# Gathering and the first expert's products in turns, in a mixture-of-experts kernel

## The chip, the cores and the metric

One NeuronCore of a Trainium2 chip runs one program. The metric is the device time of one execution in microseconds (us); lower is better. Engines are named as in the profile: PE is TensorE (PEld its weight loads), ACT is ScalarE, DVE is VectorE, POOL is GpSimd, SP is the queue that issues the weight loads. Each engine works through its own instructions strictly in program order and waits on semaphores for the others.

## The reference, cut to what matters

A trunk of four layers on 384 tokens (128 context, 256 latent) of width 1024. Each layer has a token mixer (gated DeltaNet, grouped-query attention, latent attention, DeltaNet again) and then a mixture of experts. Both are wrapped in a modulation before and a LayerNorm after. The part that the change touches is the mixture:

```python
def _moe(h, router_w, router_b, w_gate, w_up, w_down):
    scores = sigmoid(t @ router_w)                        # 16 experts, 4 groups of 4
    best_group = argmax(sum of the top-2 biased scores)   # one group for each token
    e_idx = top-2 experts inside the best group
    hid = silu(einsum("td,edf->tef", t, w_gate)) * einsum("td,edf->tef", t, w_up)
    out = einsum("tef,efd->td", hid * combine[..., None], w_down)
```

The LayerNorm is `(x - mean) * rsqrt(var + eps) * g + b` of `ALPHA * x + (1 + gate) * f(h)`.

## The kernel before, in words

**Layout.** Activations lie features by tokens: 128 partitions, 8 feature tiles, 384 columns. `bufh` holds the modulated input of a sub-layer, `bufo` the normalised values before their scale, `bufx` the residual.

**Two-part numbers.** Products of the experts are made from 32-bit values that are split into a high part (rounded to the fp32r type) and a low part (the rest). ACT copies a weight piece into `e_whi` (`split_high`, L2074, the copy's own line is L1675), then DVE subtracts it from the weight and writes `e_wlo` (`split_low`, L2802, instruction L2806). For each feature tile PE makes three products (L1495, L1498, L1499): high by high, high by low, low by high.

**Routing.** Tokens of one group are packed together. After LayerNorm, PE makes the router scores and transposes the tokens (L1555), DVE finds the group and each token's slot (`route`, L2661 to L2760), and a one-hot matrix `e_pick` says which token goes to which slot. Then every engine reads a flag and branches around a path for crowded groups (in this data the branch is not taken). DVE's first instruction after this branch is a wait at L2874.

**Gathering.** `gather_piece` (PE, L1436, instruction L1451) multiplies tokens by `e_pick`. There are eight pieces for the first pair of groups (`("G", 0, m)`). Piece m covers the feature pair q = m mod 4; pieces 0 to 3 are of the high parts, 4 to 7 of the low parts. Each is six matmuls into PSUM bank 5 or 6, and `gathered_piece` (ACT, L2059) copies the bank to `e_hs`. A piece may start when the one two before it has been copied.

**The order of the work** is the list `MOE_STEPS` for PE: first all eight `G` steps, then `U` of expert 0 (four pieces of `gate_up`, L1528, two feature tiles each, 24 column products of 512), then `W` (`pair_weights`, L1455, instruction L1462), then `U` of expert 1, and so on with `D` (down products), `T` (transposes) and `S` (scatter). ACT and DVE both follow `MOE_FOLLOW`, made from that list: `("P", j, e, p)` is the split of weight piece p, `("g", ...)` a copy of a gathered piece. Copies wait in `_open` until two pieces of the next expert stand in the list, so it begins with P0, P1, then g0 to g7, then P2, P3, P4, P5. Three pieces of split weights fit (`SPLITS`): the split of piece p waits until piece p - 3 has been used.

**Weights from memory** are loaded by SP into `ring`, eight units of 1 MB (a unit holds two pieces). A unit is loaded again when PE has used it (`ring_free`). `MOE_UNITS` is the order of these loads.

**The residual.** `scale_residual(n)` on POOL (L2924) writes ALPHA times the normalised values to `bufx`, eight instructions (L2935), one for each feature tile. It waits first for all of the next sub-layer's modulated input (`wait_all_h`, L586, called at L2932), which ACT (five tiles) and DVE (three tiles, L2252, six instructions) write, and then for each tile's `normed`, which DVE's multiply by the root (L2245) signals. It is called seven times with n above 0.

Of the kernel before, what the change touches and what calls it, by code (L numbers as in the profile page):

```python
# [28 lines left out]
P = 128  # L29
# [14 lines left out]
NE, NG, EPG = 16, 4, 4  # L44
# [48 lines left out]

MOE_STEPS = [("G", 0, m) for m in range(8)]
for _x in range(NE):
    _group, _turn = divmod(_x - 6, EPG)
    _late = _x >= 6 and _turn < 2
    if _x == 8:  # L100
        MOE_STEPS.append(("W", 1, 0))
    MOE_STEPS.append(("U", _x // EPG, _x % EPG))
    if _x == 0:
        MOE_STEPS.append(("W", 0, 0))
    if _x in (4, 5):
        MOE_STEPS += [("G", 1, 4 * (_x - 4) + m) for m in range(2)]
    if _late:
        MOE_STEPS.append(("S", _group, 2 * _turn))
    if _x >= 2:
        MOE_STEPS.append(("D", (_x - 2) // EPG, (_x - 2) % EPG))  # L110
    if _x in (4, 5):
        MOE_STEPS += [("G", 1, 4 * (_x - 4) + m) for m in range(2, 4)]
    if _late:
        MOE_STEPS.append(("S", _group, 2 * _turn + 1))
    if _x >= 1:
        MOE_STEPS.append(("T", (_x - 1) // EPG, (_x - 1) % EPG))
MOE_STEPS += [("D", 3, 2), ("T", 3, 3), ("D", 3, 3)] + [("S", 3, q) for q in range(4)]

MOE_UNITS = [(j, e, part) for kind, j, e in MOE_STEPS if kind in "UD" for part in ((0, 1) if kind == "U" else (2,))]


PIECE = UNIT // 2
# [4 lines left out]
MOE_FOLLOW, MOE_PIECE_OF = [], {}  # L127
_open, _p = [], 0
for _kind, _j, _e in MOE_STEPS:
    if _kind in "UD":  # L130
        for _k in range(4 if _kind == "U" else 2):
            MOE_FOLLOW.append(("P", _j, _e, _p))
            MOE_PIECE_OF[_kind, _j, _e, _k] = _p
            _p += 1
            if _k == 1:
                MOE_FOLLOW += _open
                _open = []
    if _kind == "W":
        _open.insert(0, ("w", _j, _e, None))
    elif _kind != "D":  # L140
        _open.append((_kind.lower(), _j, _e, None))
    elif _e == EPG - 1:
        _open.append(("y", _j, _e, None))
MOE_FOLLOW += _open
MOE_PIECES = _p
# [215 lines left out]
def trunk(nc, I, O):  # L361

    unit_at, n_units = unit_plan()
    with ExitStack() as ctx:
# [78 lines left out]
        c = Carve()  # L443
# [142 lines left out]
        def wait_all_h(eng, n):  # L586
            wait_h(eng, n, H_ACT - 1)
            wait_h(eng, n, KT - 1)
# [140 lines left out]
        def _(pe):  # L729
# [703 lines left out]
                      lambda h, kt: m_v[:, h // 2 % 2, kt, P * (h % 2):P * (h % 2) + P], fill, lambda p: None)  # L1433


            def gather_piece(l, pair, m):  # L1436

                at = 16 * l + 8 * pair + m
                half, q = divmod(m, 4)
                if m == 0:  # L1440
                    pe.wait_ge(F["pick"], 2 * l + pair + 1)
                    pe.wait_ge(tk_hi, 2 * TT * (l + 1))
                if m == 4:
                    pe.wait_ge(tk_lo, 2 * TT * (l + 1))
                if m >= 2:
                    pe.wait_ge(F["ga_ev"], at - 1)
                out = ps[:, 5 + q % 2, :].rearrange("p (g f c) -> p g f c", g=2, f=2)
                for f in range(2):
                    ft = 2 * q + f
                    for t in range(TT):  # L1450
                        last = mm(out[:, :, f, :], (e_hi, e_lo)[half][:, t, P * ft:P * ft + P], e_pick[:, t, :],  # L1451
                                  start=(t == 0), stop=(t == TT - 1))
                last.then_inc(F["ga"], 1)

            def pair_weights(l, pair, comb):  # L1455

                pe.wait_ge(comb_ready, l + 1)
                pe.wait_ge(row2_ready, l + 1)
                for g in range(2):
                    at = EPG * (2 * pair + g)  # L1460
                    for t in range(TT):
                        last = mm(ps[:, 7, 96 + 4 * g:100 + 4 * g], e_pick[:, t, P * g:P * g + P].bitcast(F32),  # L1462
                                  comb[:, t, at:at + EPG], start=(t == 0), stop=(t == TT - 1))
                last.then_inc(cs_mm, 1)
# [75 lines left out]
            def moe(l):  # L1540
# [84 lines left out]
                for kind, j, e in MOE_STEPS:  # L1625
                    n = NE * l + EPG * j + e
                    if kind == "G":
                        gather_piece(l, j, e)
                    elif kind == "W":
                        pair_weights(l, j, comb)  # L1630
                    elif kind == "U":
                        if e == 0 and j % 2 == 0:
                            pe.wait_ge(F["ga_ev"], 16 * l + 8 * (j // 2) + 8)
                        for k in range(4):
                            p = MOE_PIECE_OF["U", j, e, k]
                            gate_up(F, MOE_PIECES * l + p, p, HS_OF[j], e, k)
                    elif kind == "T":
                        transpose_hidden(F, n, e % 2)
                    elif kind == "D":
                        pe.wait_ge(F["thi"], n + 1)  # L1640
                        pe.wait_ge(F["tlo"], n + 1)
                        for k in range(2):
                            p = MOE_PIECE_OF["D", j, e, k]
                            down(F, MOE_PIECES * l + p, p, e, k)
                    else:
                        n = NG * l + j
                        if e == 0:
                            pe.wait_ge(F["ga_ev"], 16 * l + 16)
                        scatter_piece(F, n, e, e_put[:, j % 2, :], (6, 0, 1, 2) if j == NG - 1 else (5, 6),
                                      n * KT if n else None)  # L1650
# [19 lines left out]
        def _(act):  # L1670
# [385 lines left out]
                sweep(l, lambda n: m_root[:, n % TT:n % TT + 1], fill, lambda p: None)  # L2056


            def gathered_piece(l, pair, m):  # L2059
                at = 16 * l + 8 * pair + m  # L2060
                half, q = divmod(m, 4)
                act.wait_ge(F["ga"], at + 1)
                slots = e_hs[:, 0:2] if pair == 0 else e_hs[:, 0:3:2]
                copy(slots[:, :, half, 2 * q:2 * q + 2, :].rearrange("p g f c -> p g (f c)"),
                     ps[:, 5 + q % 2, :].rearrange("p (g c) -> p g c", g=2)).then_inc(F["ga_ev"], 1)

            def gathered_block(n):
                for half in range(2):
# [851 lines left out]
        def _(pool):  # L2920
# [3 lines left out]
            def scale_residual(n):  # L2924

                if n == 0:
                    wait_all_h(pool, 0)
                    for k in range(KT):
                        last = G.tensor_scalar(bufx[:, k, :], bufx[:, k, :], ALPHA, None, ALU.mult)
                    last.then_inc(ax_ready, 1)  # L2930
                    return
                wait_all_h(pool, n)  # L2932
                for k in range(KT):
                    pool.wait_ge(normed, KT * (n - 1) + k + 1)
                    last = G.tensor_scalar(bufx[:, k, :], bufo[:, k, :], x_gb[:, 0, KT * (n - 1) + k:KT * (n - 1) + k + 1],  # L2935
                                           x_gb[:, 1, KT * (n - 1) + k:KT * (n - 1) + k + 1], ALU.mult, ALU.add)
                last.then_inc(ax_ready, 1)
# [208 lines left out]
```

## Time and profile before

| what | value |
|---|---|
| three runs | 2209.02, 2210.88, 2216.32 us, median 2210.88 |
| the profiled execution's own time | 2213.71 us |
| its span, first to last instruction | 2211.9 us |
| PE busy | 2038.2 us, 92% of the span |
| DVE busy | 1339.1 us, 61% |
| ACT busy | 1034.5 us, 47% |
| POOL busy | 244.0 us, 11% |
| mean granted PE clock | 0.966 of full speed |

An engine is busy while an instruction of it runs. The granted clock is 1.00 at PE's full 2.4 GHz and 0.50 at 1.2 GHz. The gathering of the four layers begins at 510.36, 915.94, 1364.46 and 2004.63 us of the span.

### The profile page before, as it was taken

To read this page: it belongs to the slowest core of one execution; us is meant where nothing else is said; L and a number is where in the kernel's file an instruction comes from. 1 tells how busy PE (TensorE), PEld (TensorE's weight loads), DVE (VectorE), ACT (ScalarE), POOL (GpSimd) and SP (SyncE) were. 2 spreads that over 40 slices of the span, in tenths; PEclk is the share of its full clock that TensorE was granted. 3 is DMA by queue.
4 is the path that set the end of the run, shared out by engine and by line. 5 is a ranking of instruction groups with operands and counts; after the bars stand their busy time and mean duration, and the time that the engine had idled before them with its cause. 6 is when DMAs were issued, how large, how long until landed. Compare 5 with 4: busy or idle time off the path is not lost.

```text
span 2211.9 us, 44967 instructions
## 1 busy us (share of the span) xinstructions
PE 2038.2 (92%) x18880; PEld 1420.3 (64%) x18881; DVE 1339.1 (61%) x2625; ACT 1034.5 (47%) x1783; POOL 244.0 (11%) x363
## 2 busy tenths in 40 slices
PE   6999999898998999899899998998899999988996
PEld 3566666557775665677666665776466666647774
DVE  2566655437896341689722325898656666437896
ACT  3344444226774341576523315765444454226773
POOL 0432222110001000100010001000322232100000
PEclk9999999998999999899999998999999999889998
DMA  9234343345895444488643443887311121025880
GB/s 378 95 131 173 121 151 148 142 153 186 284 318 203 164 173 163 145 310 297 236 151 142 152 172 131 309 303 267 117 45 64 45 69 64 26 79 181 281 299 29
DMA packets 56768, 381.22 MB, mean 172 GB/s; under 512 B 6384, under 2 KB 10480, under 8 KB 12000
## 3 DMA queue, kind: packets, MB, share of 16 engines
q1 hardware_dynamic: 51552, 373.00, 47.2%
q10 hardware_dynamic: 4608, 4.20, 0.5%
q8 instruction: 159, 2.61, 0.5%
q0 software_dynamic: 384, 0.89, 0.1%
q14 instruction: 65, 0.53, 0.1%
HBM read 373.96 MB, written 4.10 MB: 171 GB/s over the span
## 4 chain that ended last, share of the span: by engine, by line
PE 77%; DVE 13%; ACT 5%; issue 3%; DMA 1%; SPq 0%; ACTq 0%; DVEq 0%
PE ps L834 15%; PE ps L1495 6%; PE ps L1499 5%; PE ps L1498 5%; DVE e_wlo L2806 5%; PE ps L786 4%; PE ps L762 4%; PE ps L742 3%; PE ps L974 3%; PE ps L1282 3%; DVE bufx L2824 2%; PE ps L797 2%; ACT e_whi L1675 2%; PE ps L1451 2%; PE ps L1383 2%
## 5 line engine op out<-in xcount | busy, mean ns | idle before, releaser
L2806 DVE TENSOR_TENSOR e_wlo<-ring,e_whi 128x1024 fp32r<-128x1024 f32 x384 | 456.0, 1220 | 94.6 <-ACT e_whi L1675 79.2
L1675 ACT ACTIVATE e_whi<-ring 128x1024 fp32r<-128x1024 f32 x384 | 402.9, 1060 | 120.4 <-PE ps L1499 117.2
L834 PE MATMUL ps<-bufh,ring 128*128 128x384 f32 x1024 | 394.7, 507 | 6.9 <-ACT bufo L1731 4.7
L834 PEld LDWEIGHTS ps<-bufh,ring 128*128 128x128 f32 x1024 | 177.3, 192 | 98.3 <-issue 23.3
L1495 PE MATMUL ps<-e_whi,e_hs 128*128 128x512 f32 x512 | 210.7, 412 | 28.3 <-DVE e_wlo L2806 24.8
L1675 ACT ACTIVATE scratch<-ps 128x384 f32<-128x384 f32 (+6 forms) x311 | 109.1, 368 | 220.5 <-PE ps L834 52.4
L1499 PE MATMUL ps<-e_whi,e_hs 128*128 128x512 f32 x512 | 200.8, 392 | 0.0
L1498 PE MATMUL ps<-e_wlo,e_hs 128*128 128x512 f32 x512 | 199.9, 390 | 0.0
L2935 POOL TENSOR_SCALAR bufx<-bufo,x_gb 128x384 f32<-128x384 f32 x56 | 36.2, 661 | 1104.3 <-DVE bufh L2252 1104.3
L1495 PEld LDWEIGHTS ps<-e_whi,e_hs 128*128 128x128 f32 x512 | 96.0, 188 | 69.2 <-ACT e_whi L1675 41.8
L2338 DVE SCALAR_TENSOR_TENSOR scratch<-scratch,par 128x386 f32<-128x386 f32 x192 | 128.4, 669 | 4.8
L742 PE MATMUL ps<-ring,silc 128*32 128x128 f32 x3072 | 105.8, 292 | 20.1 <-DMA ring<-in_w_ada 20.1
L1675 ACT ACTIVATE scratch<-ps,scratch 128x128 f32<-128x128 f32 x96 | 31.8, 365 | 194.6 <-PE ps L1129 192.9
L1495 PE MATMUL ps<-e_whi,e_hidT 128*128 128x512 f32 x256 | 103.2, 403 | 13.3 <-issue 9.2
L1499 PEld LDWEIGHTS ps<-e_whi,e_hs 128*128 128x128 f32 x512 | 96.0, 188 | 21.9
L742 PEld LDWEIGHTS ps<-ring,silc 128*32 128x32 f32 x3072 | 87.8, 117 | 33.8 <-DMA ring<-in_w_ada 15.6
L1498 PEld LDWEIGHTS ps<-e_wlo,e_hs 128*128 128x128 f32 x512 | 96.4, 188 | 16.6
L1675 ACT ACTIVATE lnt<-ps 128x384 f32<-128x384 f32 x26 | 12.7, 490 | 195.5 <-PE ps L797 178.6
L1498 PE MATMUL ps<-e_wlo,e_hidT 128*128 128x512 f32 x256 | 102.2, 399 | 0.0
L1499 PE MATMUL ps<-e_whi,e_hidT 128*128 128x512 f32 x256 | 101.7, 397 | 0.0
L974 PEld LDWEIGHTS ps<-scratch 32*32 32x32 f32 x6144 | 64.8, 107 | 54.7 <-issue 37.2
L2224 DVE SCALAR_TENSOR_TENSOR bufh<-ps,mod,bufx 128x128 f32<-128x128 f32 x64 | 23.4, 412 | 118.9 <-PE ps L762 77.3
(312 smaller groups left out, 3525.1 us busy)
## 6 DMA issues: line engine op xcount, KB each, us to landing
ring<-in_moe SPq DMA_DIRECT2D x192, 1024.0 KB, 4.9
ring<-in_w_ada SPq DMA_DIRECT2D x96, 1024.0 KB, 6.8
ring<-in_gdn_w_in SPq DMA_DIRECT2D x32, 1024.0 KB, 6.6
ring<-in_gdn_w_out SPq DMA_DIRECT2D x8, 1024.0 KB, 4.8
ring<-in_gqa_w_in SPq DMA_DIRECT2D x6, 1024.0 KB, 4.8
ring<-in_gqa_w_out SPq DMA_DIRECT2D x4, 1024.0 KB, 6.7
ring<-in_mla_w_out SPq DMA_DIRECT2D x4, 1024.0 KB, 7.8
ring<-in_mla_w_in SPq DMA_DIRECT2D x3, 1024.0 KB, 4.9
```

Of the source, the lines that this page charges most:

```text
L742: last = mm(ps[32 * g:32 * g + 32, bank, 0:P], silc[:, kt, :], w[:, k, g, :], start=(kt == 0), stop=(kt == KT - 1))
L762: last = mm(ps[:, banks[t % len(banks)], 0:T], w[:, t % 2, kt, :], rhs[:, kt, :], start=(kt == 0), stop=(kt == KT - 1))
L786: last = mm(ps[:, banks[t % len(banks)], 0:T], w[:, t % 2, kt, :], bufo[:, kt, :], start=(kt == 0), stop=(kt == KT - 1))
L834: last = mm(ps[:, head_bank(n, m), 0:T], w[:, m % 2, kt, :], bufh[:, kt, :], start=(kt == 0), stop=(kt == KT - 1))
L974: last = mm(ps[quarter(g), bank, at:at + 32], g_inv[a][quarter(g), d, t, :], g_inv[b][quarter(g), d, t, :], start=True, stop=True)
L1282: last = mm(ps[:, bank, 0:T], w[:, pos % 2, kt, :], bufh[:, kt, :], start=(kt == 0), stop=(kt == KT - 1))
L1495: first = mm(out, parts[0], whi, start=start, stop=False)
L1498: mm(out, parts[0], wlo, start=False, stop=False)
L1499: return mm(out, parts[1], whi, start=False, stop=stop)
L1675: return op(out, in_, ACT.Copy, **kw)
L2338: done = stt(acc, g_cin[:, m, tap:tap + CONVW], taps[:, tap:tap + 1], acc, ALU.mult, ALU.add)
L2806: return tt_(e_wlo[:, b, :], w, e_whi[:, b, :].bitcast(F32), ALU.subtract)
```

## The change

PE's order for expert 0 of each layer is now G0 G1 V0, G2 G3 V1, G4 G5 V2, G6 G7 V3, where `("V", 0, k)` is the piece k of expert 0's gate and up products. The eight gathering pieces come in the order 0, 4, 1, 5, 2, 6, 3, 7, so that the high and the low part of one feature pair stand side by side, and V k needs just these two. The lists of ACT and DVE become g0 g1 P0, g2 g3 P1, g4 g5 P2, g6 g7 P3, then P4, P5 as before. `V` waits for the copies of its two pieces. The order of the loads from memory stays the same. Apart from this, `scale_residual` no longer waits for the whole modulated input (for n above 0), only for each tile's `normed`.

```diff
--- before.py
+++ after.py
@@ -93,13 +93,15 @@
 
 
 
-MOE_STEPS = [("G", 0, m) for m in range(8)]
+GATHER_ORDER = ((0, 4, 1, 5, 2, 6, 3, 7), tuple(range(8)))
+MOE_STEPS = [step for k in range(4) for step in (("G", 0, 2 * k), ("G", 0, 2 * k + 1), ("V", 0, k))]
 for _x in range(NE):
     _group, _turn = divmod(_x - 6, EPG)
     _late = _x >= 6 and _turn < 2
     if _x == 8:
         MOE_STEPS.append(("W", 1, 0))
-    MOE_STEPS.append(("U", _x // EPG, _x % EPG))
+    if _x:
+        MOE_STEPS.append(("U", _x // EPG, _x % EPG))
     if _x == 0:
         MOE_STEPS.append(("W", 0, 0))
     if _x in (4, 5):
@@ -116,7 +118,8 @@
         MOE_STEPS.append(("T", (_x - 1) // EPG, (_x - 1) % EPG))
 MOE_STEPS += [("D", 3, 2), ("T", 3, 3), ("D", 3, 3)] + [("S", 3, q) for q in range(4)]
 
-MOE_UNITS = [(j, e, part) for kind, j, e in MOE_STEPS if kind in "UD" for part in ((0, 1) if kind == "U" else (2,))]
+MOE_UNITS = [(0, 0, 0), (0, 0, 1)]
+MOE_UNITS += [(j, e, part) for kind, j, e in MOE_STEPS if kind in "UD" for part in ((0, 1) if kind == "U" else (2,))]
 
 
 PIECE = UNIT // 2
@@ -127,6 +130,16 @@
 MOE_FOLLOW, MOE_PIECE_OF = [], {}
 _open, _p = [], 0
 for _kind, _j, _e in MOE_STEPS:
+    if _kind == "V":
+        MOE_FOLLOW.append(("P", 0, 0, _p))
+        MOE_PIECE_OF["U", 0, 0, _e] = _p
+        _p += 1
+        if _e == 3:
+            _open.append(("u", 0, 0, None))
+        continue
+    if _kind == "G" and _j == 0:
+        MOE_FOLLOW.append(("g", 0, _e, None))
+        continue
     if _kind in "UD":
         for _k in range(4 if _kind == "U" else 2):
             MOE_FOLLOW.append(("P", _j, _e, _p))
@@ -1433,18 +1446,18 @@
                       lambda h, kt: m_v[:, h // 2 % 2, kt, P * (h % 2):P * (h % 2) + P], fill, lambda p: None)
 
 
-            def gather_piece(l, pair, m):
-
-                at = 16 * l + 8 * pair + m
-                half, q = divmod(m, 4)
-                if m == 0:
+            def gather_piece(l, pair, n):
+
+                at = 16 * l + 8 * pair + n
+                half, q = divmod(GATHER_ORDER[pair][n], 4)
+                if n == 0:
                     pe.wait_ge(F["pick"], 2 * l + pair + 1)
                     pe.wait_ge(tk_hi, 2 * TT * (l + 1))
-                if m == 4:
+                if n == GATHER_ORDER[pair].index(4):
                     pe.wait_ge(tk_lo, 2 * TT * (l + 1))
-                if m >= 2:
+                if n >= 2:
                     pe.wait_ge(F["ga_ev"], at - 1)
-                out = ps[:, 5 + q % 2, :].rearrange("p (g f c) -> p g f c", g=2, f=2)
+                out = ps[:, 5 + n % 2, :].rearrange("p (g f c) -> p g f c", g=2, f=2)
                 for f in range(2):
                     ft = 2 * q + f
                     for t in range(TT):
@@ -1628,6 +1641,9 @@
                         gather_piece(l, j, e)
                     elif kind == "W":
                         pair_weights(l, j, comb)
+                    elif kind == "V":
+                        pe.wait_ge(F["ga_ev"], 16 * l + 2 * e + 2)
+                        gate_up(F, MOE_PIECES * l + e, e, HS_OF[0], 0, e)
                     elif kind == "U":
                         if e == 0 and j % 2 == 0:
                             pe.wait_ge(F["ga_ev"], 16 * l + 8 * (j // 2) + 8)
@@ -2056,13 +2072,13 @@
                 sweep(l, lambda n: m_root[:, n % TT:n % TT + 1], fill, lambda p: None)
 
 
-            def gathered_piece(l, pair, m):
-                at = 16 * l + 8 * pair + m
-                half, q = divmod(m, 4)
+            def gathered_piece(l, pair, n):
+                at = 16 * l + 8 * pair + n
+                half, q = divmod(GATHER_ORDER[pair][n], 4)
                 act.wait_ge(F["ga"], at + 1)
                 slots = e_hs[:, 0:2] if pair == 0 else e_hs[:, 0:3:2]
                 copy(slots[:, :, half, 2 * q:2 * q + 2, :].rearrange("p g f c -> p g (f c)"),
-                     ps[:, 5 + q % 2, :].rearrange("p (g c) -> p g c", g=2)).then_inc(F["ga_ev"], 1)
+                     ps[:, 5 + n % 2, :].rearrange("p (g c) -> p g c", g=2)).then_inc(F["ga_ev"], 1)
 
             def gathered_block(n):
                 for half in range(2):
@@ -2929,7 +2945,6 @@
                         last = G.tensor_scalar(bufx[:, k, :], bufx[:, k, :], ALPHA, None, ALU.mult)
                     last.then_inc(ax_ready, 1)
                     return
-                wait_all_h(pool, n)
                 for k in range(KT):
                     pool.wait_ge(normed, KT * (n - 1) + k + 1)
                     last = G.tensor_scalar(bufx[:, k, :], bufo[:, k, :], x_gb[:, 0, KT * (n - 1) + k:KT * (n - 1) + k + 1],
```

## Rows read from the trace of the kernel before

**Rows 1.** The page, busy time, share of the span, instructions: PE.

```profile
PE 2038.2 (92%) x18880; PEld 1420.3 (64%) x18881; DVE 1339.1 (61%) x2625; ACT 1034.5 (47%) x1783; POOL 244.0 (11%) x363
```

**Rows 2.** Timeline of layer 3's gathering and first expert: start, length, engine, line, count, idle before.

```profile
2004.13 1.28 ACT L1675 ACT_TABLE_LOAD   x1 [3.21 <-issue]
...
2004.63 2.90 PE L1451 MATMUL ps<-e_pick,e_hi 128*128 128x256 f32 x12 [4.24 <-issue]
...
2007.96 1.68 PE L1451 MATMUL ps<-e_pick,e_hi 128*128 128x256 f32 x12 [0.43 <-ACT e_hs L1675]
...
2009.71 3.33 PE L1451 MATMUL ps<-e_pick,e_lo 128*128 128x256 f32 x24
2010.64 2.36 DVE L2806 TENSOR_TENSOR e_wlo<-ring,e_whi 128x1024 fp32r<-128x1024 f32 x2 [3.38 <-DVEq L2873]
...
2012.36 1.32 ACT L1675 ACTIVATE e_hs<-ps 128x512 fp32r<-128x512 f32 x2 [0.34 <-PE ps L1451]
2013.58 1.05 ACT L1675 ACTIVATE e_whi<-ring 128x1024 fp32r<-128x1024 f32 x1
...
2013.73 0.50 PE L1495 MATMUL ps<-e_whi,e_hs 128*128 128x512 f32 x1 [0.69 <-ACT e_hs L1675]
...
2014.66 1.23 DVE L2806 TENSOR_TENSOR e_wlo<-ring,e_whi 128x1024 fp32r<-128x1024 f32 x1 [1.66 <-ACT e_whi L1675]
...
2017.95 2.52 DVE L2806 TENSOR_TENSOR e_wlo<-ring,e_whi 128x1024 fp32r<-128x1024 f32 x2 [0.22 <-ACT e_whi L1675]
...
2019.34 1.40 PE L1462 MATMUL ps<-lnt,e_pick 128*128 128x4 f32 x12
```

**Rows 3.** Timeline of layers 0 to 2: DVE's first split, PE's end of expert 0.

```profile
515.97 2.36 DVE L2806 TENSOR_TENSOR e_wlo<-ring,e_whi 128x1024 fp32r<-128x1024 f32 x2 [3.48 <-DVEq L2873]
...
525.83 1.40 PE L1462 MATMUL ps<-lnt,e_pick 128*128 128x4 f32 x12
...
921.98 2.36 DVE L2806 TENSOR_TENSOR e_wlo<-ring,e_whi 128x1024 fp32r<-128x1024 f32 x2 [3.41 <-DVEq L2873]
...
931.81 1.40 PE L1462 MATMUL ps<-lnt,e_pick 128*128 128x4 f32 x12
...
1370.12 2.36 DVE L2806 TENSOR_TENSOR e_wlo<-ring,e_whi 128x1024 fp32r<-128x1024 f32 x2 [3.40 <-DVEq L2873]
...
1379.66 1.40 PE L1462 MATMUL ps<-lnt,e_pick 128*128 128x4 f32 x12
```

**Rows 4.** Windows: stretch, length, busy of each engine, granted clock, DMA.

```profile
1532.50:1534.00 1.50, 0.41 (x2) 0.40 (x3) 1.50 (x5) 0.16 (x1) 0.00 (x0) 1.00 0.55 229
...
1975.00:1976.50 1.50, 0.38 (x4) 0.14 (x4) 1.50 (x3) 1.26 (x2) 0.00 (x0) 1.00 0.07 27
1976.50:1978.00 1.50, 1.50 (x10) 0.35 (x8) 1.28 (x2) 1.46 (x3) 0.00 (x0) 0.59 0.00 0
```

**Rows 5.** Waits of PE from 520 to 690 us: line, releaser, total, times, longest.

```profile
PE ps L1495 <- DVE e_wlo L2806: 6.1, 9, 1.1
```

**Rows 6.** Issues of weight loads by SP from 500 to 540 us.

```profile
L664 SPq DMA_DIRECT2D ring<-in_moe x6: 327/328/328, 522.1 to 538.1; - x6
```

**Rows 7.** Timeline of POOL and DVE after layer 0's first LayerNorm.

```profile
490.65 1.82 DVE L2252 TENSOR_SCALAR bufh<-bufo,h_gb 128x128 f32<-128x128 f32 x6
...
492.64 5.18 POOL L2935 TENSOR_SCALAR bufx<-bufo,x_gb 128x384 f32<-128x384 f32 x8 [48.62 <-DVE bufh L2252]
...
495.33 0.58 DVE L2673 TENSOR_TENSOR lnt<-lnt 128x24 f32<-128x24 f32 x1
495.83 0.17 DVE L2674 TENSOR_TENSOR lnt<-lnt 128x24 f32<-128x24 f32 x1
496.04 0.52 DVE L2677 TENSOR_TENSOR lnt<-lnt 128x12 f32<-128x12 f32 x1
...
496.75 0.45 DVE L2681 TENSOR_TENSOR lnt<-lnt 128x12 f32<-128x12 f32 x1
497.23 0.61 DVE L2683 TENSOR_TENSOR lnt<-lnt 128x12 f32<-128x12 f32 x1
```

## The prediction

> **What bounds the kernel now.** I read the page first: PE is busy 92% of the span and no other engine is near it [rows 1]. So the change can only give back PE's idle time, and it can cost time wherever it makes PE wait. Next I read the timeline of one gathering with the first expert behind it, in layer 3, line by line [rows 2], because the change reorders just this stretch, and then the same instants in layers 0 to 2 [rows 3].
>
> The reader should see four things in rows 2. First, the gathering is nearly a stream of PE work: 12 matmuls (two pieces) take 2.90 us at first and 1.68 us from 2007.96 on, and the stretch from 2004.63 to expert 0's first product at 2013.73 is 9.10 us long. Second, DVE starts its first low split only at 2010.64, 6.0 us after the gathering began. It waited for none of the others: its releaser is its own sequencer at L2873, the branch around the crowded path. Third, the splits of P0 and P1 are done in the shadow of the gathering, and P2 and P3 while PE multiplies with P0 and P1. So expert 0's products run almost without a stop from 2013.73 to 2019.34, 5.61 us, or 1.40 us a piece. Fourth, at each hand-over only one engine's latency is paid: a copy that ends at 2013.68 lets PE start at 2013.73.
>
> **The change part by part.**
>
> *The new order makes a chain.* No matmul is added or removed. But PE can go past V0 to G2 and G3 only when P0 is split, ACT splits P1 only after g3 is copied, and g3 needs PE to have finished G3, which stands behind V0. Queued behind the waiting V on PE are the next two gathering pieces, and ACT's next copy and split wait for these. So within a round nothing overlaps but the copy of the first piece of a pair. I add up a round from V(k-1)'s start to V(k)'s start, with durations of rows 2:
> - V(k-1): 1.40
> - the pair of gathering pieces: 1.68
> - from PE's end of the pair (2009.71 + 3.33 = 2013.04) to the end of the second copy (2012.36 + 1.32 = 2013.68): 0.64
> - high split, which starts 0.10 before the copy ends: 1.05 - 0.10 = 0.95
> - step to DVE 0.03, low split 1.23, step to PE 0.05: 1.31
>
> Together 5.98 us a round, in which PE stands still for 2.90 us (0.64 + 0.95 + 1.31).
>
> *The first round.* G0 and G1 end at 2004.63 + 2.90 = 2007.53. ACT's table load, which stood ahead of the first split at 2004.13, would be over at 2005.41 and stays free. Copies and high split of P0 are then done around 2009.1, but DVE comes at 2010.64 as before, since its branch isn't moved. V0 starts at 2010.64 + 1.23 + 0.05 = 2011.92, and V3 ends 3 x 5.98 + 1.40 = 19.34 us later, at 2031.26. Before, `W` began at 2019.34: 11.92 us lost. The same sum from DVE's start in the other layers [rows 3]: layer 0 515.97 gives 536.59 against 525.83, 10.76; layer 1 921.98 gives 942.60 against 931.81, 10.79; layer 2 1370.12 gives 1390.74 against 1379.66, 11.08. Sum of the four layers: **+44.6 us**, with PE at full clock.
>
> *The clock.* PE's clock falls when it has had little to do: it went from 1.00 to 0.50 in the window 1976.50 to 1978.00, after a window in which PE was busy 0.38 of 1.50 us and one like it before, while it stayed at 1.00 through 1532.50 to 1534.00, where PE was busy only 0.41 of 1.50 us but came from and went into dense work [rows 4]. The new rounds lie between the two: 3.1 us of dense work, then 2.9 us of nothing, four times, and 4.4 us of nothing ahead of V0 (2007.53 to 2011.92), at a clock that was half before the gathering began. At half clock a pair of gathering pieces takes 2.90 in place of 1.68 us, +1.22 [rows 2]. For a product piece no row at half clock exists: between nothing for waits that hide it and a doubling, +1.40, I take +1.3, as the products are wide and stand back to back. If all V and the three later pairs run at half clock: 4 x 1.3 + 3 x 1.22 = 8.9 us a layer, 35.4 in all. I take half of it, since each round's work should lift the clock part of the time and each gap should drop it: **+17.7 us**; the ends are 0 and 35.4.
>
> The Trainium skill (TensorE: Matmul & The Clock Gate, "HAM oscillation — how this bites in real kernels") says that long idle gaps of the array, repeated in every round of a loop, bring it back to the slow clock each time. By it alone the sum would take the whole 35.4 us; row 1532.50 shows a short gap survived, so I keep the half.
>
> *Weight splits ahead.* P4 and P5 now can be split during V3. Before, P4's low split began at 2017.95, well ahead of expert 1 (2019.34 plus 1.40 for `W`) [rows 2], so this gains nothing there. All waits of PE for low splits in layer 0's experts are 6.1 us in nine places [rows 5]; a fraction of one of them is the most that a head start could spare. I count nothing, bounds 0 to -1.1 a layer.
>
> *Loads.* The same units in the same order. SP issues its first new load at 522.1, when expert 0's products free unit 0 [rows 6]: the ring is full by then, so the lost time is not used for transfers and not given back by them. PE's list of waits in these experts names no DMA [rows 5]. Cost 0.
>
> *POOL's wait.* Now POOL's eight instructions (5.18 us from 492.64) start as soon as the first `normed` is there, some 5 us earlier, beside L2245 and L2252 instead of beside `route`. What sharing costs DVE in `route` can be read from [rows 7]: L2673 takes 0.58 us where L2674, of the same shape and without the hold, takes 0.17; L2677, L2681 and L2683 take 0.52, 0.45 and 0.61. Against 0.17 these four are 1.5 us longer, on the path to the first gathering. Moved away, this is up to 1.5 us gained in each of four layers, -6.0. Against it, six L2252 (1.82 us in all) now run beside POOL in seven LayerNorms. If each were held to the end of a POOL instruction (5.18/8 = 0.65 us), six would take 3.9 us, +2.1 a time, 14.6 in all; if only the first is held, at most 0.65. L2674 was let through directly behind a held one, so I take 0.8 a time, +5.6. The two nearly cancel: **0**, bounds -6 to +9 (14.6 - 6.0 = 8.6). Nobody waits for POOL's result earlier than before.
>
> The Trainium skill (GPSIMD Engine Reference, "Key points") says that GpSimd shares its SBUF interfaces with VectorE and contends with instructions that have two SBUF inputs or run in a two-port mode. The trace agrees for the first kind (0.58 against 0.17 us) [rows 7]; no row of this kernel shows L2252 beside POOL. By this rule L2252 may be held as well, which is the +9 end.
>
> Sum: 44.6 + 17.7 + 0 = 62.3 us. The profiled execution took 2213.71 us and its span 2211.9, 1 and 3 us above the median of the runs; on the profiled time it gives 2276, and on the median 2210.88 it gives **2273.2 us**, 2.8% slower.
>
> **The rivals.**
>
> *A. The chain at full clock* (0.19): the gaps of 2.9 us are survived as at 1532.50. 2210.9 + 44.6 = 2255.5. For it: dense work around each gap. Against it: the clock is already at half ahead of G0.
>
> *B. The chain at half clock all along* (0.23): 2210.9 + 44.6 + 35.4 = 2291. For it: the gaps repeat, and the first is 4.4 us. Against it: 1532.50 [rows 4].
>
> *C. The change does what its order suggests, faster* (0.04): the split of a piece is ready by the time PE reaches its V, so the products fill PE's waits in the gathering. Before, the stretch was 9.10 us long, of which the matmuls at their rate take 2.90 + 3 x 1.68 = 7.9; saving all of it is 1.2 us a layer, and with the POOL term 2210.9 - 4.8 - 6.0 = 2200.1. This decides if PE's wait ahead of each V is under some 0.3 us; my sum has 2.9. Against it: the list of ACT puts P(k) behind the copy for which PE was the only source.
>
> *D. The stall is made good later* (0.03): a fuller ring or splits done ahead remove waits of the later experts, 2211. Against it: only 6.1 us of such waits a layer, and the ring was full already [rows 5, 6].
>
> *E. A part of the chain overlaps in a way I don't see* (0.06), such as a shorter hand-over or the first round sooner: between +10 and +40, about 2236.
>
> **How the numbers follow.** The forecast (the chain, half of its work at half clock) has 0.45, A 0.19, B 0.23, C 0.04, D 0.03, E 0.06. The predicted time is the forecast's, 2273. The range reaches from A with the POOL gain and some waits spared (2248) to B with the whole POOL cost (2300). It leaves out C, D and most of E, and a little at the top. 0.3% (6.6 us) is about what a measurement of this kernel can tell from no change. Faster by more: C, 0.04. Within: D, 0.03. Slower: all the rest, 0.93.
>
> **What the changed profile would show.** Four times a layer PE idle ahead of L1495, released by DVE L2806, with about 2.9 us in rounds 1 to 3 and 4.4 us in the first; in PE's waits this pair rises by some 52 us (four times 4.4 + 3 x 2.9). Between the ends of V0 and V1 some 6 us at full clock and up to 8.6 at half. ACT idle ahead of `e_hs` copies, released by PE. DVE's first L2806 still 3.4 us behind its L2873. The start of `W` 11 to 20 us later from the start of the gathering. The granted clock near half in part of this stretch. POOL's L2935 begins within L2245; L2673 falls to about 0.17 us, and L2252 rises above its 1.82 us for six. The prediction is wrong if PE passes from G3 to V1 without a wait, or if the experts after the first run with fewer waits than before by a like amount.

## The result, and the profile after

The changed kernel takes 2282.09 us in the median of four runs (2281.18 to 2289.05), the kernel before 2210.1 on the same chip: ratio 1.0327, 95% interval 1.0299 to 1.0355, so 72 us slower. The forecast was 2273, its range 2248 to 2300.

The page after, its busy line. PE works as long as before give or take one per cent, the span is 68 us longer (line order as in [rows 1]):

```profile
span 2280.1 us, 44956 instructions
...
PE 2060.0 (90%) x18880; PEld 1436.8 (63%) x18881; DVE 1337.1 (59%) x2625; ACT 1033.2 (45%) x1783; POOL 245.9 (11%) x363
```

PE's 22 us more of busy time come with the same 18880 instructions: they ran slower. The rest is waiting. PE's waits for low splits over the whole span, before and after (line, releaser, total us, times, longest):

```profile
PE ps L1495 <- DVE e_wlo L2806: 24.8, 36, 1.1
...
PE ps L1508 <- DVE e_wlo L2822: 78.6, 53, 4.8
```

They rose by 54 us, where some 52 were forecast.

In the changed kernel L1508 is the first product of a piece, as L1495 was before, L2822 the low split (L2806), L1464 the gathering (L1451), L1475 the weights product (L1462), L1691 ACT's copies (L1675), L2950 POOL's scaling (L2935), L2268 the modulation (L2252). Layer 0's gathering and first expert after, on the timeline, to be laid beside [rows 2, 3]:

```profile
508.13 1.62 PE L1464 MATMUL ps<-e_pick,e_hi 128*128 128x256 f32 x6 [5.68 <-issue]
...
509.55 1.48 PE L1464 MATMUL ps<-e_pick,e_lo 128*128 128x256 f32 x6
...
511.07 0.60 ACT L1691 ACTIVATE e_hs<-ps 128x512 fp32r<-128x512 f32 x1 [0.68 <-PE ps L1464]
511.56 1.05 ACT L1691 ACTIVATE e_whi<-ring 128x1024 fp32r<-128x1024 f32 x1
513.50 1.22 DVE L2822 TENSOR_TENSOR e_wlo<-ring,e_whi 128x1024 fp32r<-128x1024 f32 x1 [3.47 <-DVEq L2889]
...
514.87 0.65 PE L1508 MATMUL ps<-e_whi,e_hs 128*128 128x512 f32 x1 [3.84 <-DVE e_wlo L2822]
...
518.60 0.87 PE L1464 MATMUL ps<-e_pick,e_lo 128*128 128x256 f32 x6
518.80 1.31 ACT L1691 ACTIVATE e_hs<-ps 128x512 fp32r<-128x512 f32 x2 [6.19 <-PE ps L1464]
520.00 1.05 ACT L1691 ACTIVATE e_whi<-ring 128x1024 fp32r<-128x1024 f32 x1
521.08 1.22 DVE L2822 TENSOR_TENSOR e_wlo<-ring,e_whi 128x1024 fp32r<-128x1024 f32 x1 [6.36 <-ACT e_whi L1691]
...
522.45 0.77 PE L1508 MATMUL ps<-e_whi,e_hs 128*128 128x512 f32 x1 [2.98 <-DVE e_wlo L2822]
...
530.89 0.47 PE L1508 MATMUL ps<-e_whi,e_hs 128*128 128x512 f32 x1 [2.98 <-DVE e_wlo L2822]
...
538.34 0.46 PE L1508 MATMUL ps<-e_whi,e_hs 128*128 128x512 f32 x1 [2.98 <-DVE e_wlo L2822]
...
540.55 2.56 PE L1475 MATMUL ps<-lnt,e_pick 128*128 128x4 f32 x12
```

The reader should see the same idle time, 2.98 us, ahead of V1, V2 and V3, always released by DVE's low split; ACT idle for 6.19 us until PE's gathering, and DVE idle for 6.36 us until ACT: three engines take turns. The sum had 2.90 for this gap. V0 begins one low split after DVE's branch, as worked out (513.50 + 1.22 + 0.15 us for the step to PE). The rounds are 7.58, 8.44 and 7.45 us long (514.87, 522.45, 530.89, 538.34) in place of 5.98, because a part of them ran at the lower clock. The windows of these rounds and of what follows them, after (columns as in [rows 4], last but two the granted clock):

```profile
514.87:522.45 7.58, 4.60 (x18) 3.85 (x19) 1.22 (x1) 2.14 (x3) 0.00 (x0) 0.73 0.00 0
522.45:530.89 8.44, 5.46 (x18) 4.61 (x19) 1.22 (x1) 2.14 (x3) 0.00 (x0) 0.63 0.37 124
530.89:538.34 7.45, 4.47 (x18) 3.84 (x19) 1.37 (x2) 3.54 (x5) 0.00 (x0) 0.77 0.00 0
538.34:540.55 2.21, 2.21 (x6) 1.75 (x7) 2.13 (x2) 1.77 (x2) 0.00 (x0) 0.63 0.40 70
540.55:545.00 4.45, 4.45 (x18) 4.06 (x17) 1.79 (x7) 1.33 (x2) 0.00 (x0) 0.50 0.49 203
545.00:550.00 5.00, 5.00 (x15) 3.90 (x14) 2.56 (x3) 2.11 (x2) 0.00 (x0) 0.59 0.54 170
```

The last two rows matter: the weights product and expert 1 still run at half clock, though PE no longer waits. In layers 2 and 3 it is the same (0.68 and 0.67 in the 10 us from the weights product on, 0.57 in layer 0), in layer 1 the clock was back at once (0.95).

To see where time went in all layers I read three starts in each layer from the timelines: DVE's first normalising multiply (N), the first gathering (G) and the weights product (W). Sums over the four layers in us, one profiled execution of each kernel; "order alone", "fillers" and the others are the experiments below, and the last column is layer 3's mixer, from layer 2's last N to layer 3's first:

```
kernel              N to G   G to W   W to next N   layer 3's mixer
before                91.1     61.2       723.7          423.9
changed               85.6    132.9       734.2          417.2
POOL alone            85.8     60.3       721.9          416.4
order alone           91.5    133.1       735.0          416.2
fillers               84.7    107.9       723.0          417.1
```

The routing stretch (N to G) is 5.5 us shorter, the gathering with the first expert (G to W) 71.7 us longer, the other experts 10.5 us longer. The last column is taken up at the end.

### The profile page after: what moved, and what is told of

It reads as the page before. It is cut to its first block, busy times and chain, and to the rows that moved or that the text cites. A ratio compares the mean times of both kernels' runs of the same rounds, so it can differ in the third digit from the quotient of the medians.

```text
span 2280.1 us, 44956 instructions
## 1 busy us (share of the span) xinstructions
PE 2060.0 (90%) x18880; PEld 1436.8 (63%) x18881; DVE 1337.1 (59%) x2625; ACT 1033.2 (45%) x1783; POOL 245.9 (11%) x363
## 4 chain that ended last, share of the span: by engine, by line
PE 74%; DVE 15%; ACT 5%; issue 4%; DMA 1%; SPq 0%; DVEq 0%; ACTq 0%
PE ps L847 14%; PE ps L1508 6%; DVE e_wlo L2822 6%; PE ps L1512 5%; PE ps L1511 5%; PE ps L799 4%; PE ps L775 4%; PE ps L755 3%; PE ps L987 3%; PE ps L1295 3%; DVE bufx L2840 2%; ACT e_whi L1691 2%; PE ps L810 2%; PE ps L1464 2%; PE ps L1396 2%
## 5 line engine op out<-in xcount | busy, mean ns | idle before, releaser
L2822 DVE TENSOR_TENSOR e_wlo<-ring,e_whi 128x1024 fp32r<-128x1024 f32 x384 | 456.1, 1221 | 166.8 <-ACT e_whi L1691 151.6
L1691 ACT ACTIVATE e_whi<-ring 128x1024 fp32r<-128x1024 f32 x384 | 402.2, 1059 | 129.1 <-PE ps L1512 126.2
L1508 PE MATMUL ps<-e_whi,e_hs 128*128 128x512 f32 x512 | 220.6, 431 | 78.9 <-DVE e_wlo L2822 78.6
L1512 PE MATMUL ps<-e_whi,e_hs 128*128 128x512 f32 x512 | 210.0, 410 | 0.0
L1511 PE MATMUL ps<-e_wlo,e_hs 128*128 128x512 f32 x512 | 209.1, 408 | 0.0
L1691 ACT ACTIVATE scratch<-ps 128x384 f32<-128x384 f32 (+6 forms) x311 | 109.1, 368 | 217.9 <-PE ps L847 52.8
L1508 PEld LDWEIGHTS ps<-e_whi,e_hs 128*128 128x128 f32 x512 | 100.8, 197 | 121.7 <-issue 64.0
L2950 POOL TENSOR_SCALAR bufx<-bufo,x_gb 128x384 f32<-128x384 f32 x56 | 37.6, 686 | 1137.1 <-DVE bufo L2261 1137.1
L1691 ACT ACTIVATE scratch<-ps,scratch 128x128 f32<-128x128 f32 x96 | 31.7, 364 | 189.5 <-PE ps L1142 187.8
L1512 PEld LDWEIGHTS ps<-e_whi,e_hs 128*128 128x128 f32 x512 | 101.5, 198 | 23.6
L1508 PE MATMUL ps<-e_whi,e_hidT 128*128 128x512 f32 x256 | 104.1, 407 | 13.1 <-issue 9.2
L1511 PEld LDWEIGHTS ps<-e_wlo,e_hs 128*128 128x128 f32 x512 | 101.8, 199 | 17.5
L1691 ACT ACTIVATE lnt<-ps 128x384 f32<-128x384 f32 x26 | 12.7, 490 | 196.2 <-PE ps L810 177.6
L987 PE MATMUL ps<-scratch 32*32 32x32 f32 x6144 | 76.4, 195 | 19.4 <-issue 14.3
```

The source lines that it names most:

```text
L987: last = mm(ps[quarter(g), bank, at:at + 32], g_inv[a][quarter(g), d, t, :], g_inv[b][quarter(g), d, t, :], start=True, stop=True)
L1508: first = mm(out, parts[0], whi, start=start, stop=False)
L1511: mm(out, parts[0], wlo, start=False, stop=False)
L1512: return mm(out, parts[1], whi, start=False, stop=stop)
L1691: return op(out, in_, ACT.Copy, **kw)
L2822: return tt_(e_wlo[:, b, :], w, e_whi[:, b, :].bitcast(F32), ALU.subtract)
```

## The experiments

Twelve kernels were run. "Changed" is 2282.1 us; the kernel before was timed beside each.

**POOL alone**, the kernel before with only this edit:

```diff
-                wait_all_h(pool, n)
                 for k in range(KT):
                     pool.wait_ge(normed, KT * (n - 1) + k + 1)
```

> The kernel before, with only POOL's wait for the modulated input taken away. Theory (the wait's removal is worth nothing): the four held instructions of the routing, 1.5 us a layer, are freed, 6 us in all, and the six modulating instructions of DVE take 2.7 us in place of 1.8 in seven LayerNorms, 6.3 us in all; the time is 2210 us within 3. Rival (it is a part of the loss): 2219 us or more. Other rival (it is a gain that the new order hides): 2204 us.

Measured 2202.23 against 2210.62 us, ratio 0.9958 (0.9941 to 0.9975): faster by 9.3 us, give or take 4. So the edit was a gain that the order hid, as the second rival had it. DVE's timeline in this kernel, beside [rows 7]:

```profile
492.05 2.71 DVE L2252 TENSOR_SCALAR bufh<-bufo,h_gb 128x128 f32<-128x128 f32 x6
497.34 0.21 DVE L2667 TENSOR_TENSOR lnt<-lnt,par 128x48 f32<-128x48 f32 x1 [2.59 <-ACT lnt L2099]
497.58 0.18 DVE L2673 TENSOR_TENSOR lnt<-lnt 128x24 f32<-128x24 f32 x1
...
497.90 0.17 DVE L2677 TENSOR_TENSOR lnt<-lnt 128x12 f32<-128x12 f32 x1
```

Both effects are there in the size I had given them: six L2252 take 2.71 us in place of 1.82, L2673 0.18 in place of 0.58. L2245, which has one input in PSUM, was not slowed beside POOL: eight take 3.81 us, as before (3.80). Yet the stretch N to G is 5.3 us shorter over four layers, where the two effects alone make some 2.5 (4 x 1.5 less 4 x 0.9).

**The order alone**, the changed kernel with that wait put back:

```diff
+                wait_all_h(pool, n)
                 for k in range(KT):
```

> The changed kernel with POOL's wait put back, so that only the new order of gathering, products and splits is left. Theory: all of the loss is in the order, so 2282 us within 4, and the stretch from the first gathering to the weights product L1475's line is 32 to 34 us long in each layer, as in the changed kernel. Rival (POOL beside DVE costs a part): 2275 us or less.

2291.02 us, ratio 1.0366 (1.0340 to 1.0392): 81 us slower than before, 9 more than the whole change. Loss and gain add up, 81 - 9 = 72. The theory's place for the loss held (G to W is 133.1 us, 33.3 a layer), its 2282 for the total didn't, since it took POOL's part for nothing.

**Fillers.** Matmuls that nothing reads, in the gaps:

```diff
+FILLERS = (18, 22, 22, 22)
...
                     elif kind == "V":
+                        for x in range(FILLERS[e]):
+                            mm(ps[:, 1, 0:2 * P], e_hi[:, x % TT, 0:P], e_pick[:, x % TT, :], start=True, stop=True)
                         pe.wait_ge(F["ga_ev"], 16 * l + 2 * e + 2)
```

> The changed kernel with matmuls added that nothing reads: 18 of 256 columns ahead of V0 and 22 ahead of each of V1, V2 and V3, into a PSUM bank that is free there. They fill PE's idle time ahead of each product piece (4 and 2.98 us) and change no wait for splits. Theory (a part of the loss is the clock at half level, about 71 - 45 = 27 us, and the rest is the chain): granted clock 1.00 from the second round on, rounds of 6.0 us in place of up to 8.4, time 2282 - 24 = 2258 us within 6. Rival (the clock is a bystander and the loss is the chain's hand-overs alone): 2282 us or, with the matmuls in the way, more.

2244.8 us, ratio 1.0154 (1.0126 to 1.0181): 37 us less than changed, with 84 more matmuls a layer. That is 13 us below what was expected, which had 24 us for the clock; the rival, by which nothing would come back, is out. The timeline and two windows of this kernel:

```profile
514.84 0.47 PE L1509 MATMUL ps<-e_whi,e_hs 128*128 128x512 f32 x1 [1.43 <-DVE e_wlo L2825]
...
517.74 2.80 PE L1647 MATMUL ps<-e_pick,e_hi 128*128 128x256 f32 x22
...
520.88 0.47 PE L1509 MATMUL ps<-e_whi,e_hs 128*128 128x512 f32 x1 [0.35 <-DVE e_wlo L2825]
...
526.91 0.47 PE L1509 MATMUL ps<-e_whi,e_hs 128*128 128x512 f32 x1 [0.35 <-DVE e_wlo L2825]
...
532.96 0.47 PE L1509 MATMUL ps<-e_whi,e_hs 128*128 128x512 f32 x1 [0.35 <-DVE e_wlo L2825]
```

```profile
520.00:526.00 6.00, 5.65 (x42) 5.22 (x41) 1.19 (x2) 2.14 (x3) 0.00 (x0) 1.00 0.54 175
526.00:532.00 6.00, 5.65 (x42) 5.22 (x42) 1.18 (x2) 2.58 (x4) 0.00 (x0) 1.00 0.00 0
```

The rounds are 6.04, 6.03 and 6.05 us: the chain at full clock, which the sum put at 5.98. The clock is 1.00. With POOL alone as the base, this kernel shows the chain by itself: 1.0154/0.9958 = 1.0197, 43.5 us, give or take 7 by the two intervals; the sum had 44.6.

**Fillers ahead of V3 alone**, `FILLERS = (0, 0, 0, 22)`.

> The changed kernel with 22 matmuls that nothing reads ahead of V3 alone, none ahead of V0, V1 and V2. Theory (the half clock after V3 slows the weights product and expert 1 and costs 10 us of the clock's 36): V3, the weights product and expert 1 run at full clock, the stretch from the weights product to the LayerNorm falls from 183.5 to 181 us in each layer, and 2282 - 12 = 2270 us. Rival (that stretch is longer for another reason, the splits or the ring): no change there, 2280 us.

2264.49 us, ratio 1.0240 (1.0202 to 1.0277): 17.6 us less than changed, more than was expected. G to W is 130.7 us, 2.2 less than in the changed kernel, and W to next N is 719.2, 15.0 less. So the half clock carried past V3 was the larger part of what these 22 matmuls gave back; but as fillers ahead of every V left that stretch at 723.0, some 4 us of it vary from kernel to kernel. In this kernel the weights product is at full rate right behind V3:

```profile
542.68 0.47 PE L1509 MATMUL ps<-e_whi,e_hs 128*128 128x512 f32 x1
...
544.12 1.39 PE L1476 MATMUL ps<-lnt,e_pick 128*128 128x4 f32 x12
```

**Splits ahead.** PE's order as changed, the lists of ACT and DVE set by hand:

```diff
 MOE_PIECES = _p
+MOE_FOLLOW[:12] = [P0, P1, P2, g0, g1, g2, g3, P3, g4, g5, g6, g7]
```

(each entry written out as its tuple).

> The changed kernel with PE's order untouched, but ACT and DVE split P0, P1 and P2 ahead of all copies and P3 behind g3. Theory (the chain is long because each split stands behind the copies): the wait ahead of V1 to V3 falls from 2.98 to 0.7 us, a round from 6.0 to 3.8 us at full clock; V3 ends 20 us after the first gathering, 5.3 us later than before the change; with the clock mostly full after the first round, 2210 + 21 = 2231 us, at most 2245. Rival (PE's order itself, a product between two pairs, is what costs, whatever the splits do): above 2260 us.

2233.79 us, ratio 1.0097 (1.0073 to 1.0120): 48 us less than changed. The wait ahead of V1 is now for the copy, 0.69 us, and a round at full clock is 3.78 us (527.47 to 531.25; expected 3.8):

```profile
518.21 0.77 PE L1509 MATMUL ps<-e_whi,e_hs 128*128 128x512 f32 x1 [4.11 <-DVE e_wlo L2823]
...
523.69 0.50 PE L1509 MATMUL ps<-e_whi,e_hs 128*128 128x512 f32 x1 [0.69 <-ACT e_hs L1692]
...
527.47 0.50 PE L1509 MATMUL ps<-e_whi,e_hs 128*128 128x512 f32 x1 [0.69 <-ACT e_hs L1692]
...
531.25 0.50 PE L1509 MATMUL ps<-e_whi,e_hs 128*128 128x512 f32 x1 [0.69 <-ACT e_hs L1692]
```

**One pair ahead on PE**, the lists of ACT and DVE as changed:

```diff
-MOE_STEPS = [step for k in range(4) for step in (("G", 0, 2 * k), ("G", 0, 2 * k + 1), ("V", 0, k))]
+MOE_STEPS = [G0, G1, G2, G3, V0, G4, G5, V1, G6, G7, V2, V3]
...
+MOE_FOLLOW[:12] = [g0, g1, P0, g2, g3, P1, g4, g5, P2, g6, g7, P3]
```

> The changed kernel with the lists of ACT and DVE untouched (each split behind its copies), but PE one pair ahead: G0 G1 G2 G3 V0 G4 G5 V1 G6 G7 V2 V3. Theory (it is the closed circle of gathering, copy, split and product that costs): the copies and the split of the next piece go on beside a product, V3 ends about 18 us after the first gathering in place of 32 to 34, 2210 + 13 = 2223 us within 8. Rival (the splits behind the copies cost whatever PE does): above 2250 us.

2216.3 us, ratio 1.0030 (1.0011 to 1.0048): of the change's 72 us, 66 are gone by letting PE run two gathering pieces ahead, though each split still stands behind its copies. It keeps the POOL edit, so against POOL alone it is 1.0072, some 16 us. The circle is what cost most, and either cut opens it. What stays is in G to W again, 78.2 us against 60.3 of POOL alone (88.6 in splits ahead): PE still waits there, 15.4 us in the four layers against 3.3.

**Pieces in the shadow**: POOL's wait as before, PE's order `G0 G1 G2 G3 G4 G5 G6 V0 G7 V1 V2 V3`, lists `P0 P1 g0 ... g6 P2 g7 P3`.

> The new order of features, with POOL's wait as before, but PE's order G0 to G6, V0, G7, V1, V2, V3 and the splits P0 and P1 ahead of the copies, P2 behind g6, P3 behind g7. Theory (products can start before the last copy only if no split stands in the circle): the 0.7 us of PE's wait ahead of expert 0 goes, and DVE's first low split at 6.0 us is then nearly the bound; 0.5 us a layer, 2208 us within 3, which is no difference. Rival (products among gathering pieces cost by themselves): 2215 us or more.

2207.52 against 2211.47 us, ratio 0.9975 (0.9960 to 0.9990): a small gain of about 5.5 us. The profiled execution was the slowest of the twelve (2212.13 us), so it can't show where the gain lies: G to W is 62.8 us in it against 61.2 before. Its layers differ with the clock: 14.1 us in layer 0, where the half clock ended 3.7 us behind the first gathering, 16.1 to 16.6 in the others, where it lasted 7.7 to 9.6 us. So layers compare only where the half clock ended alike. Where it ended 3.5 to 3.8 us behind the first gathering, G to W is 13.9 to 14.1 us with these orders (layer 0 here, layers 1 to 3 of the run with POOL's wait removed as well, further down) and 14.4 to 14.6 with the order of before (layer 3 of POOL alone, layers 0 and 3 of the run with POOL's wait away ahead of the experts only). That is some 0.4 us a layer, near the 0.5 expected; where the rest of the 5.5 us comes from stays open.

**POOL behind e_pick**, the kernel before with one more wait ahead of the experts:

```diff
                 wait_all_h(pool, n)
+                if n % 2:
+                    pool.wait_ge(F["pick"], n)
```

> The kernel before, in which POOL's eight instructions in the LayerNorm ahead of the experts wait in addition until DVE has made e_pick, so that they run beside neither the routing's small instructions nor the modulation. Theory (DVE's instructions with two SBUF inputs are held by POOL, 1.5 us a layer on the path to the first gathering): 2210 - 6 = 2204 us within 3. Rival (the path to the gathering is set by something else): 2210 us.

2201.9 us, ratio 0.9960 (0.9942 to 0.9977), as much as POOL alone. Here six L2252 take 1.82 us and L2673 0.18. N to G is 83.9 us, 7.2 less than before.

**POOL's wait away ahead of the experts only** (`if n % 2 == 0: wait_all_h(pool, n)`), and **ahead of the mixers only** (`if n % 2: ...`).

> The kernel before, with POOL's wait taken away only in the four LayerNorms ahead of the experts. Theory (the gain is the routing's held instructions): the whole gain of the removal, 2203 us within 3, and with the three others left alone perhaps a little less. Rival (POOL's earlier end helps the mixers): 2210 us.

> The kernel before, with POOL's wait taken away only in the three LayerNorms ahead of a mixer. Theory (nothing there waits for POOL, and DVE's six modulating instructions take 0.9 us longer each time, part of it on the path): 2211 to 2213 us, no difference. Rival (this is where the gain came from): 2205 us or less.

Ahead of the experts: 2199.54 us, ratio 0.9947 (0.9929 to 0.9966), 11.7 us. Ahead of the mixers: 2209.19 us, ratio 0.9987 (0.9965 to 1.0010), no difference. So the gain comes from the wait in the four LayerNorms ahead of the experts. N to G is 83.1 us with it away there, 8.0 less than before, and 92.8 with it away ahead of the mixers only.

**Both together**: pieces in the shadow with POOL behind e_pick, and with POOL's wait removed.

> The last two together: pieces in the shadow and POOL behind e_pick. Theory: the two gains add, 2202 us within 4. Rival: the earlier gathering meets DVE's branch end, so that only one of them counts, 2206 us.

> Pieces in the shadow of the gathering, as in the run with G0 to G6, V0, G7, V1, V2, V3, together with the change's removal of POOL's wait. Theory: the removal is worth the 9 us that it was worth alone, and the pieces 4: 2198 us within 4, the same as with POOL behind e_pick. Rival (both shorten the same path): 2203 us.

2197.78 us, ratio 0.9938 (0.9916 to 0.9960), and 2195.75 us, ratio 0.9945 (0.9925 to 0.9965). Both are faster than both kernels, by 12 to 14 us against the one before; they don't differ from each other, nor clearly from POOL's wait away ahead of the experts alone.

## Why the prediction was right, step by step

**The chain** was right in kind and size. A round was put at 5.98 us with a gap of 2.90; measured 6.04 at full clock and gaps of 2.98. The sum of 44.6 us stands against 43.5 by the runs, and 46.7 by the stretch G to W (107.9 with fillers, less 61.2). Splits ahead and one pair ahead show that the circle made most of it, and not the placing of a product among gathering pieces.

**The clock** was right in kind and too small: 17.7 us taken, 37.3 measured (2282.1 - 2244.8), just over the upper end of 35.4. The term was mis-sized twice. Inside the rounds, G to W shrinks from 132.9 to 107.9 with fillers: 25.0 us where I had 17.7. And the term stopped at V3, while the half clock didn't: W to next N is 734.2 against 723.0 us, 11.2 us more. In layer 0 the clock was at 0.50 from 539 to 549 us, through the weights product (2.56 us in place of 1.40) and most of expert 1's gate and up products. The end of 35.4 was itself a little high: a product piece at half clock, six matmuls 0.43 us apart, takes 2.56 us, +1.16 in place of the +1.3 taken, which makes 33.2 us for all rounds at half. Against this the 25.0 say that some three quarters of the rounds' work ran at half clock, where I took half.

The reading of [rows 4] on which I took the half doesn't hold either. I wrote that PE came to 1532.50 from dense work; the window just before it shows that it didn't (first the one ahead of the row 1975.00, then this one):

```profile
1973.50:1975.00 1.50, 0.69 (x2) 0.08 (x1) 0.77 (x1) 0.00 (x0) 0.00 (x0) 1.00 1.03 437
...
1531.00:1532.50 1.50, 0.29 (x3) 0.06 (x1) 1.50 (x4) 1.17 (x2) 0.00 (x0) 1.00 0.91 382
```

PE was busy 0.70 of 3.00 us there and the clock stayed at 1.00; in the 3.00 us ahead of 1976.50 it was busy 1.07 us, and the clock fell. These rows don't tell which gaps are survived, so the half was a guess between the two ends. The Trainium skill (TensorE: Matmul & The Clock Gate, "HAM oscillation — how this bites in real kernels") tells of a loop whose waits of some 3 to 5 us bring the clock down in each round. Here the waits inside the rounds were 2.98 us, and the trace agrees in part: the windows of the three rounds have 0.73, 0.63 and 0.77, so the clock fell again and again, but not for the whole of a round. That 37.3 lies near the 35.4 that I had as the end by this rule is chance, since 11.2 of it came from behind the rounds.

**POOL's wait** was the step that failed: 0 taken with -6 as its end, -9.3 measured (interval -13 to -5.5). Its two parts had the right size on DVE, the hold on the routing gone and +0.9 us on the six modulating instructions. But it was counted in seven LayerNorms (at 0.8 each), and with the wait away ahead of the mixers only, no cost shows (0.9987). And the sum left out PE's clock between N and G.

PE's first product that needs the routing (L1570, in the changed kernel L1583) waits for DVE's `e_rs`. Its wait before, four times 3.1 us in the mean:

```profile
PE ps L1570 <- DVE e_rs L2696: 12.5, 4, 3.3
```

and after, 1.7, as in POOL alone:

```profile
PE ps L1583 <- DVE e_rs L2712: 6.9, 4, 1.7
```

The wait is shorter from both sides: `e_rs` comes some 0.6 us sooner, and the work ahead of it on PE ends some 0.9 us later, since it needs the modulated input. In POOL alone L1570 so starts 2.5 us earlier behind N, over four layers. The rest is in PE's matmuls from L1570 on, until DVE's L2726 starts, which waits for a part of them. These are layer 1's windows, before:

```profile
905.04:910.25 5.21, 5.21 (x25) 5.21 (x26) 2.95 (x10) 1.79 (x3) 0.00 (x0) 0.50 0.00 0
```

and in POOL alone:

```profile
901.16:905.03 3.87, 3.87 (x25) 3.56 (x26) 2.96 (x10) 1.74 (x3) 0.00 (x0) 0.76 0.00 0
```

Over the four layers this stretch takes 5.21, 5.21, 5.21 and 3.53 us before, and 4.45, 3.87, 5.21 and 2.80 in POOL alone, at granted clocks of 0.50, 0.50, 0.50, 0.76 and 0.62, 0.76, 0.50, 1.00: 2.8 us less with the same work. 2.5 and 2.8 are the 5.3 of N to G. No run changed the clock there by itself, but the profiles sort by the wait ahead of L1570: in the four kernels with 2.8 to 3.5 us of it in every layer (the one before, order alone, pieces in the shadow, wait away ahead of the mixers) the four stretches take 19.2 to 20.9 us together, in the ten with 1.7 us 14.1 to 17.5 us. The +0.9 us is on the path: with POOL behind e_pick, where L2252 isn't slowed, L1570 starts 10.50 us behind N in layer 0, in POOL alone 11.39, before 12.04. The other 4 us of the measured 9.3 I can't place with one profile of each kernel; layer 3's mixer, taken up at the end, is a candidate.

The Trainium skill (GPSIMD Engine Reference, "Key points") names two kinds of VectorE instructions that contend with GpSimd. For those with two SBUF inputs the trace agrees again: L2673 takes 0.58 us beside POOL and 0.18 with POOL moved away. For the kind in a two-port mode it can't be said: L2252 beside POOL takes 2.71 us in place of 1.82, but no row shows the mode in which it ran.

**Splits ahead of expert 1 and the loads** gave nothing back, as said: W to next N with fillers is 723.0 us, before 723.7.

Of the cases, the chain came true with more of its work at half clock than the forecast, between it and B. That the likeliest time was 9 us low is two errors that partly cancel: the clock 20 us too small, POOL 9 us too high. One slip without effect: it is the profiled execution that lay 3 us above the median, and its span 1 us.

## What to carry to other kernels

When work on three engines is put "in turns", write down for one round who is waited for by whom: if the last step of round k must come before the first of round k + 1 on the same in-order engine, the round costs the sum of its steps, and one pair of work run ahead on that engine is the cure (here it took away 66 of the 82 us by which the changed kernel lies above POOL alone). Count the clock of TensorE as a part of every gap's price, also in the work behind the last gap. A wait of an engine off the path can be worth more where it ends than where it stands: ask which instructions run beside its work, and what gap of TensorE they make longer.

## What the runs showed of the hardware that was not expected

**Half clock in dense work.** After the last gap in layer 0 PE was busy all the time, and still at half level for some 10 us. Windows of the changed kernel:

```profile
537.50:539.00 1.50, 0.66 (x3) 0.61 (x4) 1.50 (x2) 1.48 (x3) 0.00 (x0) 0.97 0.00 0
539.00:541.00 2.00, 2.00 (x8) 1.62 (x7) 1.47 (x2) 1.34 (x2) 0.00 (x0) 0.50 0.57 131
...
547.00:549.00 2.00, 2.00 (x6) 1.60 (x5) 1.23 (x1) 0.47 (x1) 0.00 (x0) 0.50 0.87 221
549.00:551.00 2.00, 2.00 (x10) 1.57 (x9) 1.23 (x1) 1.35 (x2) 0.00 (x0) 0.97 0.75 311
```

The clock was back 10.8 us behind V3's start in layer 0, 9.1 and 9.3 us behind it in layers 2 and 3, but 3.5 us behind it in layer 1, with the same work in the same order. What makes the difference was not tried.

**A stage that the change doesn't touch moves by 8 us.** Layer 3's mixer took 423.9 us in the profile of before and 416.2 in that of the order alone, both with POOL's wait. In the 30 us that begin 360 us into it the clock was 0.72 before and 1.00 in POOL alone. First before, then POOL alone:

```profile
1919.30:1949.30 30.00, 28.03 (x115) 19.36 (x115) 10.70 (x28) 3.25 (x9) 1.56 (x4) 0.72 0.05 13
```

```profile
1915.00:1945.00 30.00, 28.51 (x135) 18.65 (x136) 11.39 (x29) 3.15 (x9) 1.56 (x4) 1.00 0.22 75
```

So a difference of a few us between two profiled spans of this kernel may be the clock's luck in a stage far from the edit; the median of many runs, or the same stretch in both, has to decide. Whether POOL's wait makes the fall in that mixer more likely is open: of the profiles with the wait ahead of the experts five have 420.9 us or more and one 416.2, of the eight without it all have 420.1 or less (421.8 and 417.4 us in the mean).
